# A hybrid decoder layer on one core: one residual add moved ahead of a normalisation on VectorE, and two blocks of router products reordered on TensorE

## The chip, the cores and the metric

The kernel runs on one core of one Trainium2 chip. The metric is the device time of one execution in microseconds; three runs of the kernel before are given. Everything is float32. A float32 product of TensorE appears in the profile as two matmul records (an output of 128x512 as "128x512 f32 x2").

## The reference

One step of one decoder layer, for 256 prompt tokens and 8 sample tokens (264 rows, D = 1024): RMSNorm, one input projection, dilated attention and RWKV-7 mixing side by side, a gated merge, an output projection with residual add; then RMSNorm, and a mixture of 32 experts of which each token takes four. What follows the merge is what matters here:

```
x = x + mixed @ w_out
h = rmsnorm(x, ln2)
logits = h @ w_router + b_router              # (264, 32)
top_v, top_i = top_k(logits, 4);  gate = softmax(top_v)
# per expert e, for the tokens that chose it:
gu  = h @ w_gate_up[e] + b_gate_up[e]         # 1024 -> 2048
act = (min(max(up, -7), 7) + 1) * (gt * sigmoid(1.702 * gt)),  gt = min(gt, 7)
x  += gate[e] * (act @ w_down[e] + b_down[e]) # 1024 -> 1024
y = rmsnorm(x, ln_f)
```

## The kernel before

The program of each engine is written out by hand, in its own block: TensorE (`pe`), VectorE (`dve`), ScalarE (`act`), GpSimd (`pool`), and SyncE (`sp`), which issues nearly all loads. No scheduler changes the order; an engine runs its instructions as they are written, and `wait_ge` on a semaphore holds back everything behind it on that engine.

The 264 rows form three tiles: m = 0 and 1 with 128 prompt rows each, m = 2 with the 8 sample rows. They are treated in the order `MORDER` = (2, 0, 1), so norm2(0) is the second RMSNorm of tile 2, norm2(1) that of tile 0, norm2(2) that of tile 1; residual(m) and logits(m) take the tile itself.

PSUM has eight banks. The list `psum_jobs` gives each product a bank in turn; `give(job)` waits until the job before in this bank is read out, `done` tells that the bank is full, `take` waits for that, and `free` tells that it is read out.

Around the change the work is as follows.
- Output projection: `out_projection(m, g)` makes 128 rows by 512 columns of `mixed @ w_out` (8 products, line 1550). VectorE adds it to the residual stream `acc` in `residual(m)` (a 128x512 add for each g, line 811). The sample tile has its own packed product (line 1578), and four adds of 8x512.
- Norm: ScalarE squares `acc` and takes the root (`rms2`, lines 659 and 660), VectorE takes the reciprocal (line 1105) and scales into `h2` (line 1106). Before rms2 of tile 0, ScalarE waits for the h2 of the sample rows and copies these rows of `acc` (line 671).
- Router: TensorE transposes h2 in blocks of 128 columns (`h2_T`, line 1246), ScalarE copies the result out (line 515), TensorE multiplies with w_router (`logits`, line 1569), VectorE takes the four largest (`route`, lines 1115 to 1118, semaphore `sel_r`), ScalarE the exponentials, VectorE the gates (`gates`, lines 1133 to 1135, semaphore `gate`).
- Ranks: products of the selection with constant matrices count the tokens ahead of each one for its expert (job `rk`, lines 1611 to 1622). From them VectorE builds `sel` (line 1153), which says which token sits in which of 64 slots of an expert.
- Sample gates: they are transposed and placed (lines 1616 and 1618) in bank BX, and read from there by ScalarE and VectorE.
- `open_sum(m, g)` (line 1601) copies a 128x512 piece of `acc` by a product with the identity into a PSUM bank, in which the experts' results are summed later.
- `gather` (line 1637) brings the tokens of an expert pair into the slots, `bias` (line 1646) opens the sums of the expert product.
- Expert loop: 32 turns (line 1686 gate and up, line 1697 transposes, line 1714 down, line 1669 the combination of the expert before).

The weights of an expert come in six units of 2 MB, four of w_gate_up and two of w_down, into a ring of eight buffers. The issue of unit n waits for the semaphore `unit_used` to reach n + 1 (line 489); the loop raises it by one for each unit that TensorE has consumed, and ahead of the loop it is raised by 3, 3 and 2 as buffers that held other weights come free, the last two behind wo10 and wo11.

Of the kernel before, what the change touches and what calls it, by code (L numbers as in the profile page):

```python
# [19 lines left out]
NB = 8  # L20
# [12 lines left out]
NE = 32  # L33
# [92 lines left out]
def build(nc, A, O):  # L126
# [5 lines left out]
    BG, BU, BY, BX = [bank[j] for j in ("rk", "ro1", "ht11", "ht10")]  # L132
    BA = ((bank["ro2"], bank["ro0"]), (bank["ht01"], bank["wo11"]))

    with ExitStack() as ctx:
# [3 lines left out]
        def sem(name):  # L139
            return ctx.enter_context(nc.semaphore(name))  # L140
# [3 lines left out]
        PS = [ctx.enter_context(nc.psum_tensor(f"ps{b}", [128, 512], F32)) for b in range(8)]  # L144
# [19 lines left out]
        C = {n: mats[:, i, :] for i, n in enumerate(CONST_NAMES)}  # L164
# [142 lines left out]
        gate = place(NM, NE)  # L307
# [18 lines left out]
        def S_(name):  # L326
            if name not in SEM:
                SEM[name] = sem(name)
            return SEM[name]

        def take(eng, job):
            eng.wait_ge(full[bank[job]], turn[job])

        def after(eng, *names):
            for job in names:
                eng.wait_ge(evac[bank[job]], turn[job])

        def psum(job, *dims, parts=128):
            return view(PS[bank[job]], 0, *dims)[:parts]
# [466 lines left out]
        def _(dve):  # L806
# [3 lines left out]
            def tt(out, a, b, op):  # L810
                return v.tensor_tensor(out, a, b, op)  # L811
# [276 lines left out]
            def residual(m):  # L1088
                n = ROWS[m]
                a = lambda g: acc[:n, m, g * 512:(g + 1) * 512]  # L1090
                if m == 2:
                    take(dve, "wo2")
                    for j in range(4):
                        ins = tt(a(j % 2), PS[bank["wo2"]][32 * j:32 * j + n, :], a(j % 2), ALU.add)
                        V.free(ins, "wo2") if j == 3 else V(ins)
                else:
                    for g in range(2):
                        take(dve, f"wo{m}{g}")
                        V.free(tt(a(g), psum(f"wo{m}{g}", 512, parts=n), a(g), ALU.add), f"wo{m}{g}")

            def norm2(i):
                m = MORDER[i]
                n = ROWS[m]
                dve.wait_ge(S_("rms2"), i + 1)
                V(v.reciprocal(rs1[:n, m:m + 1], rs1[:n, m:m + 1]))
                V.ready(v.scalar_tensor_tensor(h2[:n, m, :], acc[:n, m, :], rs1[:n, m:m + 1], ln2b[:n], ALU.mult, ALU.mult),
                        "h2", i + 1)
# [11 lines left out]

            dve.wait_ge(S_("ld_acc"), 48)  # L1120
            residual(2)
            dve.wait_ge(S_("ld_ln2"), 16)
            norm2(0)
            residual(0)
            norm2(1)
            residual(1)
            def gates(i):
# [72 lines left out]
            last = dve.snap(passes * NE)  # L1200
# [29 lines left out]
        def _(pe):  # L1230
            mm = nc.tensor.matmul

            def give(job):

                if turn[job] > 1:
                    pe.wait_ge(evac[bank[job]], turn[job] - 1)

            def done(ins, job):
                ins.then_inc(full[bank[job]], 1)

            def transposes(job, pieces, width, parts=128):

                give(job)
                for n, src in enumerate(pieces):
                    rows = src.shape[0]
                    last = nc.tensor.transpose(PS[bank[job]][:parts, n * width:n * width + rows], src, C["ident"][:rows, :rows])  # L1246
                done(last, job)
# [80 lines left out]
            for h in range(H):  # L1328
# [4 lines left out]
                if h % 2:  # L1333
                    job = f"ov{h // 2}"
                    give(job)
                    for hh in (h - 1, h):
# [3 lines left out]
                        last = mm(psum(job, S)[q, 128:256], vn[:, 1, hh * 64:hh * 64 + 64], ptb[:, hh % 2, 256:384], start=False, stop=True)  # L1340
# [9 lines left out]
                if h == 3:  # L1350
# [3 lines left out]
                    for t in range(3):  # L1354
                        last = nc.tensor.transpose(PS[bank["sst"]][:64, KO[t]:KO[t] + KT[t]], scs[:KT[t], t, :], C["ident"][:KT[t], :KT[t]])
                    done(last, "sst")
                if h == 6:
# [3 lines left out]
                    for t in range(3):  # L1361
                        last = nc.tensor.transpose(PS[bank["spt"]][:KT[t], t * 64:t * 64 + 64], s64[:64, KO[t]:KO[t] + KT[t]], C["ident"][:64, :64])
# [7 lines left out]
            for c in range(4):  # L1370
                for g in range(2):
                    last = mm(psum("sv", 4, 2, 4)[:, c, g, :], pvm[:, g, c * 128:(c + 1) * 128], C["quad"][:, 0:4], start=True, stop=True)
# [35 lines left out]
            def prod(lhs, rhs):  # L1408
# [20 lines left out]
                                                     start=True, stop=True), "Auk")  # L1429
            heads("MT", prod(aA2, aI), "LX2", "X2T")  # L1430
            for pr in range(2):
                after(pe, f"MT{pr}", f"AV{pr}")
                for m in range(2):
                    job = f"HG{pr}{m}"
                    give(job)
                    for hh in range(4):
                        for r in range(2):
                            a, b = AV[half(r), pr, m, hh, :], natK[half(r), m, head(pr, hh)]
                            both = bass.AP(a.tensor, a.offset, [list(a.ap[0]), [b.offset - a.offset, 2], [1, 64]])
                            last = mm(psum(job, 4, 128)[half(r), hh, :], aA2T[half(r), pr, m, hh, :], both, start=True, stop=True)  # L1440
# [3 lines left out]
            for r in range(2):  # L1444
                job = f"Y0{r}"
                give(job)
                for m in range(2):
                    for hh in range(4):
                        for pr in range(2):
# [4 lines left out]
                            last = mm(out, HG[half(r), pr, m, hh, 0:64], aBrb[half(r), pr, m, hh, :], start=False, stop=True)  # L1454
                done(last, job)
            for r in range(2):
                job = f"Rp{r}"
                give(job)
                for m in range(2):
                    for hh in range(4):  # L1460
                        for pr in range(2):
                            last = mm(psum(job, 2, 4, 64)[half(pr), m, hh, :], HG[half(r), pr, m, hh, 64:128],
                                      aBrb[half(r), pr, m, hh, :], start=True, stop=True)
# [49 lines left out]
            for c in range(1, NCH):  # L1513
                job = f"yt{c}"
                give(job)
                for hh in range(4):
                    for pr in range(2):
                        last = mm(psum(job, 4, CH)[half(pr), hh, :], stc[c - 1][half(pr), hh, :], Rp[half(pr), hh, c * CH:(c + 1) * CH],
                                  start=True, stop=True)
# [16 lines left out]
            for c in range(4):  # L1536
                pe.wait_ge(S_("obT"), c + 1)
                for d in range(KD):
                    if c == 0:
                        give(f"mb{d}")  # L1540
                    last = mm(psum(f"mb{d}", T), wb[:, c, d * 128:(d + 1) * 128], YT[:, c, :], start=c == 0, stop=c == 3)  # L1541
# [12 lines left out]
            def half(rows, u, j):  # L1554

                return rows[:, u * 256 + j:u * 256 + 256:2]

            def h2_T(i):
                m = MORDER[i]
                pe.wait_ge(S_("h2"), i + 1)  # L1560
                for g in range(2):
                    transposes(f"ht{m}{g}", [half(h2[:ROWS[m], m, :], 2 * g + c // 2, c % 2) for c in range(4)], ROWS[m])

            def logits(m):
                n = ROWS[m]
                after(pe, f"ht{m}0", f"ht{m}1")
                give(f"ro{m}")
                for k in range(KD):
                    last = mm(psum(f"ro{m}", NE, parts=n), h2T[:, k, m * 128:m * 128 + n], wr[:, k, :], start=k == 0, stop=k == KD - 1)
                done(last, f"ro{m}")  # L1570
# [3 lines left out]
            for k in range(4):  # L1574
                pe.wait_ge(S_("mix"), 2 * k + 2)
                for j in range(4):
                    kk, g = 2 * k + j // 2, j % 2
                    last = mm(PS[bank["wo2"]][32 * j:32 * j + NB, :], mixT[:, kk, S:T], wo[:, kk, g * 512:(g + 1) * 512],
                              start=k == 0, stop=k == 3)
# [15 lines left out]
            def bank_free(b):  # L1595
                pe.wait_ge(evac[b], max(turn[j] for j in jobs if bank[j] == b))

            def open_sum(m, g):

                bank_free(BA[m][g])  # L1600
                mm(PS[BA[m][g]][:, :], C["ident"], acc[:, m, g * 512:(g + 1) * 512], start=True, stop=False)

            open_sum(1, 0)
            open_sum(1, 1)
            h2_T(2)
            open_sum(0, 0)
            logits(1)
            give("rk")
            rk = psum("rk", 3, NE)
            pe.wait_ge(S_("sel_r"), 2)  # L1610
            mm(rk[:, 0, :], C["before"], selr[:, 0, :], start=True, stop=False)
            mm(rk[:, 1, :], C["ones"], selr[:, 0, :], start=False, stop=False)
            mm(rk[:, 2, :], C["ones"], selr[:, 0, :], start=False, stop=False)
            pe.wait_ge(S_("gate"), 1)
            bank_free(BX)
            nc.tensor.transpose(PS[BX][0:NE, 0:NB], gate[:NB, 2, :], C["ident"][:NB, :NB])
            for g in range(2):
                last = mm(PS[BX][g * 64:g * 64 + 64, 64:64 + NE], C["idstack"][0:NB, 0:64], gate[:NB, 2, :], start=True, stop=True)
            last.then_inc(S_("gate_s_full"), 1)
            pe.wait_ge(S_("sel_r"), 3)  # L1620
            mm(rk[:, 1, :], C["before"], selr[:, 1, :], start=False, stop=False)
            done(mm(rk[:, 2, :], C["ones"], selr[:, 1, :], start=False, stop=True), "rk")
# [5 lines left out]
            for g in range(2):  # L1628
                q = slice(g * 64, g * 64 + NE)
                last = mm(PS[BY][g * 64:g * 64 + NB, :], gsT[q], yS[q, :], start=True, stop=True)  # L1630
# [27 lines left out]
            for m in range(2):  # L1658
                last = nc.tensor.transpose(PS[BY][0:NE, m * 128:(m + 1) * 128], gate[:, m, :], C["ident"])
# [67 lines left out]
            for m in range(2):  # L1727
                for g in range(2):
                    q = slice(g * 64, g * 64 + 64)
                    last = mm(PS[BA[m][g]][:, :], selgT[q, m * 128:(m + 1) * 128], yS[q, :], start=False, stop=True)  # L1730
                last.then_inc(S_("cmb_full"), 1)
            pe.wait_ge(S_("samp_sq"), 1)
            for g in range(2):
                last = mm(PS[BX][g * 64:g * 64 + 64, 0:1], C["idstack"][:, 0:64], sqs, start=True, stop=True)
# [23 lines left out]
```

## Time and profile before

| | us |
|---|---|
| median of three runs | 1331.39 |
| lowest, highest | 1330.75, 1335.32 |
| the profiled execution, its own time | 1331.39 |
| its span in the trace | 1329.5 |
| TensorE busy | 1222.0 (92%) |
| VectorE busy | 337.6 (25%) |
| ScalarE busy | 200.7 (15%) |
| mean granted TensorE clock, share of full | 0.981 |

The span is cut into three parts: the mixers and the projection up to about 380 us, the router up to about 400 us, and the 32 experts from there to the end. The page's view of 40 equal slices shows it for DMA:

```profile
DMA  8357565414498999999999999999999999999994
GB/s 276 122 176 170 195 212 143 146 35 166 164 390 333 427 429 427 429 429 427 429 429 427 429 429 427 429 429 427 429 429 427 429 430 427 429 430 427 429 429 173
```

Each column is 33.2 us. TensorE's busy share is an average over records that overlap, so it doesn't tell by itself that TensorE sets the end.

### The profile page before, as it was taken

The page shows a single profiled execution, that of the slowest core. Times are in us where ns is not written, and L with a number is a line of the kernel's source. Part 1 is how long each engine was busy: PE and PEld are TensorE (multiplying, and loading weights), DVE is VectorE, ACT ScalarE, POOL GpSimd, SP SyncE. Part 2 cuts the span into 40 slices and gives each one's busy share as a digit, 9 for nine tenths or more (in the row PEclk, how much of TensorE's full clock was granted, in tenths as well). Part 3 has the DMA queues.
Part 4 walks back from the last instruction along what each step waited for, and adds up shares of the span by engine and source line. Part 5 has one row for each costly group of instructions (what it writes and reads, how often), then busy time and mean ns, then how long its engine had stood idle before and what let it go on. Part 6 is the DMA issues. An engine that isn't in the chain of part 4 may idle for free.

```text
span 1329.5 us, 18567 instructions
## 1 busy us (share of the span) xinstructions
PE 1222.0 (92%) x7636; PEld 605.2 (46%) x7636; DVE 337.6 (25%) x649; ACT 200.7 (15%) x401; POOL 79.2 (6%) x48
## 2 busy tenths in 40 slices
PE   5999968898999999999999998999999989999996
PEld 5888854886553334333333333333333333333332
DVE  3042756735541112111211111121111112111112
ACT  2113423222121001001011000110010010101002
POOL 0000070550000000000000000000000000000001
PEclk9999987899989999999999999999999999999998
DMA  8357565414498999999999999999999999999994
GB/s 276 122 176 170 195 212 143 146 35 166 164 390 333 427 429 427 429 429 427 429 429 427 429 429 427 429 429 427 429 429 427 429 430 427 429 430 427 429 429 173
DMA packets 52510, 460.03 MB, mean 346 GB/s; under 512 B 7922, under 2 KB 10300, under 8 KB 27884
## 3 DMA queue, kind: packets, MB, share of 16 engines
q1 hardware_dynamic: 49252, 451.45, 82.1%
q0 software_dynamic: 1888, 5.34, 2.1%
q10 hardware_dynamic: 1328, 2.64, 0.6%
q8 instruction: 31, 0.51, 0.2%
q14 instruction: 11, 0.09, 0.0%
HBM read 454.27 MB, written 5.11 MB: 346 GB/s over the span
## 4 chain that ended last, share of the span: by engine, by line
PE 60%; DMA 27%; DVE 4%; issue 3%; ACT 3%; POOL 1%; SPq 1%; DVEq 0%; ACTq 0%; POOLq 0%
PE ps L1686 21%; DMA work<-in_w_gate_up 13%; DMA ring<-in_w_gate_up 13%; PE ps L1714 12%; PE ps L1271 8%; PE ps L1637 4%; PE ps L1669 2%; PE ps L1550 2%; PE ps L1246 2%; PE ps L1646 2%; PE ps L1490 1%; PE ps L1409 1%; POOL ring L761 1%; PE ps L1541 1%; DVE ring L811 1%
## 5 line engine op out<-in xcount | busy, mean ns | idle before, releaser
L1686 PE MATMUL ps<-ring,work 128*64 128x512 f32 x1536 | 341.8, 595 | 20.6 <-DMA ring<-in_w_gate_up 20.2
L1686 PEld LDWEIGHTS ps<-ring,work 128*64 128x64 f32 x1536 | 107.4, 137 | 252.2 <-issue 217.2
L1714 PE MATMUL ps<-ring,work 128*64 128x512 f32 x768 | 170.1, 595 | 18.4 <-ACT work L717 18.4
L1271 PE MATMUL ps<-work,ring 128*128 128x264 f32 x672 | 150.3, 386 | 0.7 <-DVE work L811 0.7
L1180 DVE TENSOR_SCALAR work<-ps 128x512 f32<-128x512 f32 x32 | 22.1, 692 | 466.9 <-PE ps L1686 466.9
L1271 PEld LDWEIGHTS ps<-work,ring 128*128 128x128 f32 x672 | 127.4, 190 | 22.5 <-DVE work L811 0.8
L1686 PE MATMUL ps<-work 128*64 128x512 f32 x512 | 114.3, 596 | 6.2 <-DMA work<-in_w_gate_up 6.2
L1714 PEld LDWEIGHTS ps<-ring,work 128*64 128x64 f32 x768 | 53.4, 137 | 119.7 <-issue 104.0
L1199 DVE SCALAR_TENSOR_TENSOR work<-work 128x512 f32<-128x512 f32 x32 | 24.1, 752 | 309.8 <-ACT work L720 309.8
L712 ACT ACTIVATE work<-work 128x512 f32<-128x512 f32 x32 | 20.1, 629 | 503.1 <-DVE work L1180 503.1
L1637 PEld LDWEIGHTS ps<-work 128*128 128x128 f32 x544 | 68.2, 200 | 29.9 <-DVE work L1184 15.2
L1637 PE MATMUL ps<-work 128*128 128x128 f32 x544 | 74.7, 292 | 2.0
L811 DVE TENSOR_TENSOR work<-work 128x512 f32<-128x512 f32 (+7 forms) x73 | 61.5, 843 | 50.8 <-ACT work L515 45.0
L1686 PEld LDWEIGHTS ps<-work 128*64 128x64 f32 x512 | 35.2, 137 | 84.3 <-issue 69.3
L1669 PE MATMUL ps<-work 64*128 64x512 f32 x256 | 63.6, 615 | 0.0
L802 POOL TENSOR_SCALAR work<-work 8x512 f32<-8x512 f32 x2 | 3.1, 1561 | 1011.4 <-DVE work L1221 1011.3
L1714 PE MATMUL ps<-work 128*64 128x512 f32 x256 | 56.7, 595 | 5.9 <-ACT work L717 5.9
L720 ACT ACTIVATE work<-ps 128x512 f32<-128x512 f32 x32 | 19.1, 597 | 230.6 <-PE ps L1714 230.6
L515 ACT ACTIVATE work<-ps 128x264 f32<-128x264 f32 (+6 forms) x63 | 26.5, 421 | 159.6 <-PE ps L1271 123.4
L1669 PEld LDWEIGHTS ps<-work 64*128 64x128 f32 x256 | 22.0, 186 | 41.1 <-issue 41.1
L1646 PE MATMUL ps<-work 32*64 32x512 f32 x264 | 35.9, 613 | 0.0
L1714 PEld LDWEIGHTS ps<-work 128*64 128x64 f32 x256 | 17.6, 137 | 39.9 <-issue 32.1
(250 smaller groups left out, 913.8 us busy)
## 6 DMA issues: line engine op xcount, KB each, us to landing
ring<-in_w_gate_up SPq DMA_DIRECT2D x96, 2048.0 KB, 31.1
ring<-in_w_down SPq DMA_DIRECT2D x48, 2048.0 KB, 35.2
work<-in_w_gate_up SPq DMA_DIRECT2D x32, 2048.0 KB, 30.9
work<-in_w_down SPq DMA_DIRECT2D x16, 2048.0 KB, 34.7
ring<-in_w_in SPq DMA_DIRECT2D x6, 3072.0 KB, 16.0
ring<-in_w_out SPq DMA_DIRECT2D x1, 4096.0 KB, 14.0
ring<-in_w_in SPq DMA_DIRECT2D x2, 1536.0 KB, 9.1
ring<-in_cache_k SPq DMA_DIRECT2D x16, 192.0 KB, 3.3
```

The costliest lines, as they stand in the source:

```text
L515: A_.free(nc.scalar.activation(dst, src, func, **kw), job)
L811: return v.tensor_tensor(out, a, b, op)
L1180: v.tensor_scalar(gt, PS[BG][:, :], LIMIT, None, ALU.min).then_inc(S_("gt"), 1)
L1199: v.scalar_tensor_tensor(accs, yS, gsamp[:, bass.ds(it, 1)], accs, ALU.mult, ALU.add).then_inc(S_("samp_out"), 1)
L1246: last = nc.tensor.transpose(PS[bank[job]][:parts, n * width:n * width + rows], src, C["ident"][:rows, :rows])
L1271: last = mm(psum(job, T), WIN[gi % 2][:, k, j * 128:(j + 1) * 128], hT[:, k, :], start=k == 0, stop=k == KD - 1)
L1550: last = mm(psum(job, 512), mixT[:, k, m * 128:m * 128 + 128], wo[:, k, g * 512:(g + 1) * 512], start=k == 0, stop=k == KD - 1)
L1637: last = mm(PS[BX][:, c * 128:(c + 1) * 128], h2[:, m, half * 512 + (c // 2) * 256 + c % 2:half * 512 + (c // 2 + 1) * 256:2], sel[:, m].r ...
L1646: mm(PS[(BG, BU)[i]][g * 64:g * 64 + 64, :], pick[q, :], ebias[q, g * 512:(g + 1) * 512], start=True, stop=False)
L1669: mm(PS[BA[m][g]][:, :], selgT[q, m * 128:(m + 1) * 128], yS[q, :], start=False, stop=False)
L1686: last = mm(PS[bnk][g * 64:g * 64 + 64, :], lhs, UNIT[n % 8][:, w0 + base + g * 512:w0 + base + (g + 1) * 512], start=False, stop=k == KD - 1)
L1714: last = mm(PS[BY][g * 64:g * 64 + 64, :], lhs, UNIT[n % 8][:, w0:w0 + 512], start=k == 0, stop=k == KD - 1)
```

## The change

On VectorE, residual(0) moves from behind norm2(0) to directly behind residual(2). On TensorE, logits(1) moves ahead of open_sum(0, 0), and the transpose and placement of the sample gates move ahead of `give("rk")` and the first three rank products. The list of PSUM jobs, ScalarE, GpSimd and SyncE are the same.

```
             residual(2)
+            residual(0)
             dve.wait_ge(S_("ld_ln2"), 16)
             norm2(0)
-            residual(0)
             norm2(1)
             residual(1)
...
             open_sum(1, 1)
             h2_T(2)
+            logits(1)
             open_sum(0, 0)
-            logits(1)
+            pe.wait_ge(S_("gate"), 1)
+            bank_free(BX)
+            nc.tensor.transpose(PS[BX][0:NE, 0:NB], gate[:NB, 2, :], C["ident"][:NB, :NB])
+            for g in range(2):
+                last = mm(PS[BX][g * 64:g * 64 + 64, 64:64 + NE], C["idstack"][0:NB, 0:64], gate[:NB, 2, :], start=True, stop=True)
+            last.then_inc(S_("gate_s_full"), 1)
+
             give("rk")
             rk = psum("rk", 3, NE)
             pe.wait_ge(S_("sel_r"), 2)
             mm(rk[:, 0, :], C["before"], selr[:, 0, :], start=True, stop=False)
             mm(rk[:, 1, :], C["ones"], selr[:, 0, :], start=False, stop=False)
             mm(rk[:, 2, :], C["ones"], selr[:, 0, :], start=False, stop=False)
-            pe.wait_ge(S_("gate"), 1)
-            bank_free(BX)
-            nc.tensor.transpose(PS[BX][0:NE, 0:NB], gate[:NB, 2, :], C["ident"][:NB, :NB])
-            for g in range(2):
-                last = mm(PS[BX][g * 64:g * 64 + 64, 64:64 + NE], C["idstack"][0:NB, 0:64], gate[:NB, 2, :], start=True, stop=True)
-            last.then_inc(S_("gate_s_full"), 1)
             pe.wait_ge(S_("sel_r"), 3)
```

VectorE's instructions between the end of the sample residual and the scaling of tile 0, as a difference (ps5 and ps6 hold the two halves of out_projection(0); the four adds ahead of them are residual(2)):

```order
 L811 TENSOR_TENSOR work<-ps4,work 8x512 x4
+L811 TENSOR_TENSOR work<-ps5,work 128x512
+L811 TENSOR_TENSOR work<-ps6,work 128x512
 L1105 RECIPROCAL work<-work 8x1
 L1106 SCALAR_TENSOR_TENSOR work<-work 8x1024
-L811 TENSOR_TENSOR work<-ps5,work 128x512
-L811 TENSOR_TENSOR work<-ps6,work 128x512
 L1105 RECIPROCAL work<-work 128x1
 L1106 SCALAR_TENSOR_TENSOR work<-work 128x1024
```

The two adds that read the first tile's projection stand ahead of the reciprocal and scaling of the eight sample rows now.

TensorE's instructions from the second half of the transposes of tile 1 to the last rank product, before (ps5 is the bank of open_sum(0, 0), ps1 that of logits(1), ps2 that of the ranks, ps7 that of the sample gates):

```order
 L1246 MATMUL ps0<-work 128x128 x4
 L1601 MATMUL ps5<-work 128x512
 L1569 MATMUL ps1<-work 128x32 x8
 L1611 MATMUL ps2<-work 128x32
 L1612 MATMUL ps2<-work 128x32
 L1613 MATMUL ps2<-work 128x32
 L1616 MATMUL ps7<-work 32x8
 L1618 MATMUL ps7<-work 64x32 x2
 L1621 MATMUL ps2<-work 128x32
 L1622 MATMUL ps2<-work 128x32
```

and in the changed kernel, where the lines behind 1601 have moved by up to 6 with the code:

```order
 L1246 MATMUL ps0<-work 128x128 x4
 L1569 MATMUL ps1<-work 128x32 x8
 L1601 MATMUL ps5<-work 128x512
 L1610 MATMUL ps7<-work 32x8
 L1612 MATMUL ps7<-work 64x32 x2
 L1618 MATMUL ps2<-work 128x32
 L1619 MATMUL ps2<-work 128x32
 L1620 MATMUL ps2<-work 128x32
 L1622 MATMUL ps2<-work 128x32
 L1623 MATMUL ps2<-work 128x32
```

The product of 512 columns stands behind the logits instead of ahead of them, and the gate pieces stand between it and the ranks.

## Rows read from the trace of the kernel before

**Rows 1.** Chain that ended last: start us, us, what.

```profile
738.23 33.07 DMA ring<-in_w_gate_up
1299.91 3.65 PE ps L1686 x16
```

**Rows 2.** Windows: from:to, length, busy (x instructions) by engine, clock, DMA share, GB/s.

```profile
390.00:392.00 2.00, 2.00 (x6) 0.36 (x7) 1.40 (x7) 1.15 (x6) 0.00 (x0) 0.56 0.96 397
396.00:398.00 2.00, 2.00 (x15) 1.20 (x13) 1.73 (x9) 0.54 (x1) 0.00 (x0) 0.73 0.14 57
402.00:404.00 2.00, 2.00 (x14) 0.58 (x10) 0.00 (x0) 1.41 (x3) 0.00 (x0) 1.00 0.00 0
440.00:480.00 40.00, 38.31 (x198) 15.65 (x196) 8.00 (x19) 4.54 (x9) 0.00 (x0) 1.00 1.01 428
```

**Rows 3.** Timeline of SyncE's queue at 380 and 404: start us, us, what.

```profile
380.68 0.91 SPq L489 DMA_DIRECT2D ring<-in_w_gate_up  x2
...
404.33 3.77 SPq L489 DMA_DIRECT2D ring<-in_w_gate_up  x2
```

**Rows 4.** Timeline of TensorE, output projection: start us, us, what.

```profile
349.73 14.00 PE L1550 MATMUL ps<-ring,work 128*128 128x512 f32 x32
363.66 1.12 PE L1246 MATMUL ps<-work 8*128 8x8 f32 x8
364.71 7.13 PE L1550 MATMUL ps<-ring,work 128*128 128x512 f32 x16
```

**Rows 5.** Timeline of VectorE, same stretch.

```profile
356.31 1.27 DVE L1106 SCALAR_TENSOR_TENSOR work<-work 8x1024 f32<-8x1024 f32 x1
...
363.84 0.69 DVE L811 TENSOR_TENSOR work<-ps,work 128x512 f32<-128x512 f32 x1 [5.53 <-PE ps L1550]
366.20 0.16 DVE L1105 RECIPROCAL work<-work 128x1 f32<-128x1 f32 x1 [1.67 <-ACT work L660]
366.40 1.28 DVE L1106 SCALAR_TENSOR_TENSOR work<-work 128x1024 f32<-128x1024 f32 x1
```

**Rows 6.** Timeline of ScalarE, the copies of the sample rows.

```profile
357.70 1.29 ACT L671 ACTIVATE work<-work 8x512 f32<-8x512 f32 x2 [1.71 <-DVE work L1106]
```

**Rows 7.** Timeline of TensorE, from the router to the first expert.

```profile
384.73 1.02 PE L1601 MATMUL ps<-work 128*128 128x512 f32 x2
385.83 1.94 PE L1569 MATMUL ps<-work 128*128 128x32 f32 x16
...
389.51 0.41 PE L1621 MATMUL ps<-work 128*128 128x32 f32 x2 [0.73 <-DVE work L1118]
...
389.98 1.79 PE L1601 MATMUL ps<-work 128*128 128x512 f32 x2
391.70 1.88 PE L1630 MATMUL ps<-work 32*8 32x512 f32 x4
393.51 3.75 PE L1637 MATMUL ps<-work 128*128 128x128 f32 x16
...
398.20 2.15 PE L1637 MATMUL ps<-work 128*128 128x128 f32 x16
...
400.50 1.08 PE L1686 MATMUL ps<-ring,work 128*64 128x512 f32 x4
```

**Rows 8.** Timeline of TensorE, the longest wait shortly before the change.

```profile
328.10 2.29 PE L1541 MATMUL ps<-work,ring 128*128 128x264 f32 x6 [4.49 <-issue]
```

**Rows 9.** Windows of two earlier stretches.

```profile
190.00:212.00 22.00, 15.09 (x52) 8.93 (x52) 18.38 (x32) 9.66 (x28) 6.85 (x2) 0.50 0.95 270
328.00:334.00 6.00, 5.90 (x19) 4.83 (x20) 5.76 (x8) 0.00 (x0) 0.00 (x0) 0.72 0.45 175
```

**Rows 10.** Timeline of VectorE, sel and the last gates.

```profile
391.27 1.12 DVE L1153 TENSOR_SCALAR work<-work 128x64 f32<-128x64 f32 x4
...
397.08 0.24 DVE L1135 TENSOR_SCALAR work<-work 128x32 f32<-128x32 f32 x1
```

## The prediction

> **What bounds the kernel now.** I read the chain of waits first, because the change sits in front of a long loop and only the chain says what that loop is worth. From 400 us on the kernel runs 32 experts, each with 12 MB of weights. Up to 738 us the chain runs on TensorE; from there it is made mostly of weight transfers, the first of 33.07 us, and the last of them releases TensorE at 1299.9 us, some 30 us before the end [rows 1]. So the end is set by the weight stream: a fixed number of bytes at a fixed rate, counted from the moment at which the stream last stood still.
>
> The windows show where that is. The DMA share falls to 0.14 in 396 to 398 us and is 0.00 in 402 to 404 us; in 440 to 480 us it is 1.01 at 428 GB/s, and the transfers in the chain say that it stays so [rows 1, 2]. The reason is the ring of eight weight buffers. Eight units were queued before the loop, the last two at 380.68 us; the ninth is issued at 404.33 us, when TensorE has consumed the first unit of the first expert [rows 3]. TensorE reaches this expert at 400.50 us [rows 7]. Therefore each microsecond by which TensorE enters the expert loop later or earlier moves the end by a microsecond, until the hole in the stream (396 to 404 us, some 8 us) is closed. The question is only what the change does to 400.50 us.
>
> **The change part by part.** There are two independent edits.
>
> First edit, VectorE: residual(0) now stands ahead of norm2(0). norm2(0) makes the eight sample rows of h2, which TensorE transposes (the eight L1246 at 363.66 us) between the two halves of the output projection. Before, its scaling (1.27 us) was over at 357.58 us, 6 us ahead of its reader, under out_projection(0, 0) and (0, 1), which run from 349.73 for 14.00 us [rows 4, 5]. residual(0) needs both of these products; its second half cannot start before TensorE has finished the second, and starts at 363.84 us [rows 5]. What was hidden now stands bare behind it: 363.84 + 0.69 (second half of the residual) + 0.16 (reciprocal, priced by the next one) + 1.27 (scaling) + 0.04 twice between them (366.20 + 0.16 to 366.40) = 366.04. With 0.1 us for the signal and the weight load in front of the first transpose, an estimate, that is 366.1 to 366.2. TensorE is in order and waits there from 363.66: **+2.5 us**. Queued behind the waiting transposes is out_projection(1, 0), 7.13 us [rows 4], and behind it everything up to the loop.
>
> The other engines follow, and I looked for a second delay. ScalarE waits for the same h2, copies the sample rows (1.29 us [rows 6]) and only then squares tile 0: it starts that at about 367.4 us instead of 364.6. From the square to VectorE's reciprocal it took 1.6 us before (366.20 [rows 5]), so norm2(1) ends near 370.5 us. Its reader, the transposes of tile 0, comes after out_projection(1, 0), at 366.18 + 1.1 + 7.1 = 374.3 us. That leaves 3.8 us: no second stall. The last two weight units are issued 2.5 to 4 us later than 380.68, while the first six (12.6 MB, 29 us at 428 GB/s from 357 us) are still under way until 386: nothing. The gain that one might look for in the first edit, banks of PSUM freed earlier, is nothing either: TensorE shows no wait for such a bank in this stretch.
>
> TensorE's clock adds a term. The nearest rows of a stall are those before 328.10 us, 4.49 us of idleness [rows 8]; the granted clock behind it is 0.72 over 328 to 334 us [rows 9], and as the clock has only the levels 2.4 and 1.2 GHz, (1 - 0.72) x 2 x 6 = 3.4 us of these are at 1.2. On the other side, short waits in the loop (1.7 us of 40 not busy) leave the clock at 1.00 [rows 2]. The new stall of 2.5 us has 1.05 us of transposes of eight columns directly behind it, so it is nearer to the former. A spell of 3.4 us at half clock over dense work loses 1.7 us. The bounds are 0 (none) and 3.4 us (6.8 us at half clock, the length of the spell near 391 us, below). I take **+1.7**, with a little over even odds.
>
> The Trainium skill says in "TensorE: Matmul & The Clock Gate", part 1, "the default state is throttled, and activity releases the throttle". By that rule the stall can cost more than its own length, and the sum is the +1.6 below; with no loss of clock it would be -0.1. The trace of before agrees with the direction: half clock follows its pauses.
>
> Second edit, TensorE: logits(1) moves ahead of open_sum(0, 0), and the transpose and the two placements of the sample gates move ahead of the first three rank products. open_sum used to fill the 0.9 us in which ScalarE evacuates the transposed rows (L1601 at 384.73, logits at 385.83 us [rows 7]). Now TensorE is idle there, logits(1) starts at the same time, and open_sum(0, 0) takes its 0.9 us after it. Before, TensorE had done three rank products and the gate pieces and waited 0.73 us until 389.51 for the third selection from VectorE [rows 7]. The moved open_sum fills this wait: the last rank product comes at most 0.2 us later. VectorE's route and gates don't wait for any of it and keep their pace, and sel, which the gather needs, is ready at 392.39 us (391.27 + 1.12) as before [rows 10]: **0** in the first place.
>
> But again the clock. In before, the stretch 385.8 to 390.0 us holds only products of 32 columns or fewer and the wait, and at 390 to 392 us the granted clock is 0.56, at 396 to 398 us 0.73, so at 1.2 GHz from 390.2 to 397.1, 6.8 us [rows 2]. In it the open_sum took 1.79 us (1.02 at 384.73), the sample bias 1.88 and the gather 3.75 (2.15 for the next one at full clock) [rows 7]. After the change the thin stretch is cut by a dense product in its middle. If that keeps the clock at 2.4 GHz, open_sum and bias end at about 392.1; the gather waits for sel and starts at 392.5 instead of 393.51 (-1.0) and takes 1.6 us less: **-2.6 us**. More isn't to be had: the gates of tile 1 are ready at 397.32 us, just under the new entry at 397.9 [rows 10]. If the spell comes all the same the term is 0 to +0.2. I take -2.6 at about two to one; the change leaves less thin work together than before, but adds 0.9 us of idleness next to it.
>
> Sum: 2.5 + 1.7 - 2.6 = **+1.6 us** on the end. The profiled execution took 1331.39 us (span 1329.5 and 1.9 around it), and that is also the median of the three runs. Forecast: **1333.0 us**.
>
> **The rivals.** What a measurement of this kernel can tell from no change is about 0.5%, or 6.7 us; nearly all cases below lie within it.
> - A, the forecast: stall, one short spell at half clock behind it, the later spell gone. 1333.0 us, chance 0.36.
> - B, no spell behind the stall, the later one gone: 2.5 - 2.6 = -0.1, 1331.3 us. For it: the stall is little more than half as long as the one before 328.10 us. Chance 0.28.
> - C, a spell in both places: 2.5 + 1.7 + 0.2 = +4.4, 1335.8 us. For it: clock changes follow pauses with some scatter, and the second edit opens a new pause of 0.9 us. Chance 0.18.
> - D, a spell only in the later place: +2.7, 1334.1 us. Chance 0.13.
> - E, slower than can be overlooked: the clock doesn't come back within 3.4 us but stays at half over the whole of out_projection(1, 0), as it stayed for 22 us at 190 to 212 us [rows 9]. Price: 2.5 + 7.1 (that projection doubled) + 0.2 = +9.8, 1341.2 us. It decides the verdict once more than some 8 us of dense work run at half clock. Against it: in that stretch TensorE was busy for 15.1 of 22 us in small pieces, whereas here 7 us of dense products follow at once. Chance 0.04.
> - F, faster by over 0.5%: the hole in the weight stream is 8 us, so it isn't excluded by the bandwidth, but no term gives more than -2.6 us. Even without the stall (VectorE's order forbids that) the time would be 1328.8 us, 0.2% less; only a long spell at half clock that the profile of before doesn't show could bring more. Chance 0.01.
> - That the shift doesn't reach the end at all (the stream has slack somewhere else) gives 1331.4 us as B does. Against it is the DMA share of 1.01 right behind the hole.
>
> **How the numbers follow.** The likeliest is A, so 1333.0. A to D lie from 1331.3 to 1335.8; with 1.3 us below for a spell in the profile of before that other runs may not have, and 1 us above for two spells longer than taken, the range is 1330.0 to 1336.8. Faster 0.01 (F), slower 0.04 (E), the same 0.95.
>
> **What would show it.** In the profile after: the eight transposes of the sample rows start 2.4 to 2.6 us after the second product of out_projection(0), with VectorE named as releaser; VectorE's scaling of eight rows comes after the two residual halves. No wait of TensorE before the transposes of tile 0. A clock under 1.00 somewhere in 366 to 371 us in case A or C, and none between the logits of tile 1 and the expert loop in A or B. The entry into the expert loop at 402.1 (A), 400.4 (B), 404.9 (C) or 403.2 us (D), the ninth weight unit issued 3.8 us later, and the last transfer's end moved by the same amount. The prediction is wrong in its core if the entry moves and the end doesn't, or if the entry moves by more than 6 us.

## The result and the profile after

| | before | after |
|---|---|---|
| median, us | 1332.08 (16 runs) | 1339.05 (16 runs) |
| lowest to highest | 1328.23 to 1336.39 | 1337.70 to 1341.85 |
| mean granted TensorE clock, profiled execution | 0.981 | 0.977 |
| ratio after / before | | 1.0051, 95% interval 1.0041 to 1.0060 |

The change costs 7 us, 0.51%. I had forecast +1.6 us and a range up to 1336.8, so the time lies outside. Of the 6.05 us between the forecast of 1333.0 and the median of 1339.05, 0.7 us is the base: I had counted from 1331.39, three runs, and the median of 16 is 1332.08. The other 5.4 us is the change itself, +7.0 instead of +1.6.

The profiled execution of the changed kernel took 1340.89 us, 9.5 us more than that of before. 2.5 us of these lie ahead of everything that the change touches: out_projection(0, 0) starts at 352.24 us instead of 349.73. This start varies from execution to execution: over the eleven profiles of this case it lies between 343.94 and 352.69 us, and at both ends of this for one and the same kernel (e4 and e7 below). All positions are therefore counted from the start of out_projection(0, 0) from here on, called P. The expert loop is entered at P + 50.77 before and P + 57.78 after: +7.01 us, which is the whole of the loss. The names in the rows: ps is a bank of PSUM, work and ring are buffers in SBUF, and L1550 is a line of kernel.py; behind line 1601 the numbers differ by up to 6 from those of before, as the code has moved. TensorE's timeline of the changed kernel, answering to [rows 4, 7] (start us, us, what, and in brackets the idle time before and who ended it):

```profile
352.24 14.00 PE L1550 MATMUL ps<-ring,work 128*128 128x512 f32 x32
368.59 1.12 PE L1246 MATMUL ps<-work 8*128 8x8 f32 x8 [2.35 <-DVE work L1106]
369.64 10.05 PE L1550 MATMUL ps<-ring,work 128*128 128x512 f32 x16
...
393.68 1.94 PE L1569 MATMUL ps<-work 128*128 128x32 f32 x16 [0.95 <-ACT work L515]
395.46 1.52 PE L1601 MATMUL ps<-work 128*128 128x512 f32 x2
...
397.39 0.64 PE L1618 MATMUL ps<-work 128*128 128x32 f32 x2
...
399.11 0.61 PE L1623 MATMUL ps<-work 128*128 128x32 f32 x2
399.54 2.05 PE L1601 MATMUL ps<-work 128*128 128x512 f32 x2
401.52 1.88 PE L1631 MATMUL ps<-work 32*8 32x512 f32 x4
403.33 3.44 PE L1638 MATMUL ps<-work 128*128 128x128 f32 x16
```

The reader is to see three things. The transposes of the sample rows wait 2.35 us for VectorE's scaling; they stand at P + 16.35 instead of P + 13.93, 2.42 us later. out_projection(1, 0) behind them takes 10.05 us instead of 7.13: 2.92 us. And the stretch from logits(1) at 393.68 to open_sum(0, 1) at 399.54 takes 5.86 us, where it took 4.15 before (385.83 to 389.98 [rows 7]): another 1.7 us. The five rank products start 0.43 us apart (397.39 to 399.11) in it, where at full clock they stand 0.22 us apart (e6 below shows it). With the new order and full clock the stretch takes 4.30 us (e2 below), so 0.15 of the 1.7 us is the order and 1.56 the clock. 2.42 + 2.92 + 1.7 = 7.0.

VectorE in the same execution, answering to [rows 5, 10]:

```profile
366.35 0.69 DVE L811 TENSOR_TENSOR work<-ps,work 128x512 f32<-128x512 f32 x1 [6.17 <-PE ps L1550]
367.07 0.15 DVE L1105 RECIPROCAL work<-work 8x1 f32<-8x1 f32 x1
367.26 1.27 DVE L1106 SCALAR_TENSOR_TENSOR work<-work 8x1024 f32<-8x1024 f32 x1
371.55 0.16 DVE L1105 RECIPROCAL work<-work 128x1 f32<-128x1 f32 x1 [3.02 <-ACT work L660]
371.75 1.28 DVE L1106 SCALAR_TENSOR_TENSOR work<-work 128x1024 f32<-128x1024 f32 x1
...
399.84 0.42 DVE L1150 SCALAR_TENSOR_TENSOR work<-ps,work 128x32 f32<-128x32 f32 x2 [1.20 <-PE ps L1623]
400.29 1.12 DVE L1153 TENSOR_SCALAR work<-work 128x64 f32<-128x64 f32 x4
```

and the instruction of line 1150 in the kernel before:

```profile
390.82 0.42 DVE L1150 SCALAR_TENSOR_TENSOR work<-ps,work 128x32 f32<-128x32 f32 x2
```

The second half of the residual, reciprocal and scaling follow each other without a hole, as worked out. New is the wait of 1.20 us for the last rank product. It costs nothing, though: `sel` (line 1153) is ready at 401.41, and the gather that needs it starts at 403.33, directly behind the sample bias on TensorE. The 1.7 us are TensorE's own, spent in its queue at half clock.

The windows of the changed kernel, answering to [rows 2] (from:to, length, busy by engine, granted clock, DMA share, GB/s):

```profile
366.00:368.00 2.00, 0.24 (x1) 0.00 (x0) 1.58 (x3) 0.00 (x0) 0.00 (x0) 1.00 1.00 426
368.00:376.00 8.00, 7.41 (x16) 3.74 (x17) 1.98 (x3) 3.10 (x7) 0.00 (x0) 0.57 1.01 430
376.00:394.00 18.00, 17.05 (x80) 9.68 (x79) 4.74 (x16) 4.24 (x8) 0.00 (x0) 1.00 0.99 411
396.00:406.00 10.00, 10.00 (x35) 5.79 (x34) 6.55 (x30) 1.57 (x7) 0.00 (x0) 0.50 0.44 184
406.00:408.00 2.00, 2.00 (x16) 1.07 (x15) 1.44 (x8) 0.54 (x1) 0.00 (x0) 0.94 0.00 0
```

Behind the stall the clock is 0.57 over 8 us: (1 - 0.57) x 2 x 8 = 6.9 us at 1.2 GHz; in the profile of before the clock is 1.00 from P + 14 to P + 40.5. In the router it is 0.50 for all of 396 to 406 us and a little beyond, 10.2 us where [rows 2] gave 6.8. It begins 3.2 us later from P than before (P + 43.8 against P + 40.5), but earlier in the program: in open_sum(0, 0), ahead of the rank products, and not behind them. And the end follows the entry:

```profile
413.86 3.77 SPq L489 DMA_DIRECT2D ring<-in_w_gate_up  x2
```

```profile
1309.43 3.65 PE ps L1687 x16
```

The first is SyncE's issue of the ninth weight unit (404.33 before [rows 3]; +9.5 with the 2.5 of the late start), the second the piece of the chain released by the last weight transfer (1299.91 before [rows 1]). From the entry into the loop to this piece are 1309.43 - 410.02 = 899.41 us after, and 1299.91 - 400.50 = 899.41 us before.

### The profile page after: what moved, and what is told of

It reads as the page before. It is cut to its first block, busy times and chain, and to the rows that moved or that the text cites. A ratio compares the mean times of both kernels' runs of the same rounds, so it can differ in the third digit from the quotient of the medians.

```text
span 1339.0 us, 18567 instructions
## 1 busy us (share of the span) xinstructions
PE 1229.0 (92%) x7636; PEld 609.7 (46%) x7636; DVE 337.6 (25%) x649; ACT 200.9 (15%) x401; POOL 79.1 (6%) x48
## 4 chain that ended last, share of the span: by engine, by line
PE 61%; DMA 27%; DVE 4%; issue 3%; ACT 3%; POOL 1%; SPq 1%; DVEq 0%; ACTq 0%; POOLq 0%
PE ps L1687 20%; DMA work<-in_w_gate_up 13%; DMA ring<-in_w_gate_up 13%; PE ps L1715 12%; PE ps L1271 8%; PE ps L1638 4%; PE ps L1550 2%; PE ps L1670 2%; PE ps L1647 2%; PE ps L1246 2%; PE ps L1409 1%; PE ps L1490 1%; PE ps L1541 1%; DVE ring L811 1%; ACT work L689 1%
## 5 line engine op out<-in xcount | busy, mean ns | idle before, releaser
L811 DVE TENSOR_TENSOR work<-work 128x512 f32<-128x512 f32 (+7 forms) x73 | 61.5, 842 | 52.9 <-ACT work L515 47.1
L1687 PEld LDWEIGHTS ps<-work 128*64 128x64 f32 x512 | 35.2, 137 | 84.3 <-issue 69.3
L1246 PE MATMUL ps<-work 128*128 128x128 f32 (+4 forms) x141 | 22.3, 311 | 15.2 <-DMA work<-in_r_k 12.8
```

Source lines behind the costliest of these rows:

```text
L1687: last = mm(PS[bnk][g * 64:g * 64 + 64, :], lhs, UNIT[n % 8][:, w0 + base + g * 512:w0 + base + (g + 1) * 512], start=False, stop=k == KD - 1)
```

## The experiments

My theory after the result: the first edit costs the stall (2.4) and 2.9 for half clock behind it; the remaining 1.7 is the clock in the router. What it doesn't tell is to which edit the last term belongs. "Entry" is the first product of the expert loop from P in the one profiled execution; the timed ratio is against the kernel before, run beside it on the same chip; its median there was 1332.87 us (29 runs, for e1 to e4), 1331.83 (23, for e5 to e8) and 1332.78 (17, for e9), so the medians of the table can't be subtracted across these groups.

| kernel | entry | half clock behind P + 14 | median, us (runs) | ratio, 95% interval |
|---|---|---|---|---|
| before | 50.77 | 6.8 us from P + 40.5 | 1332.08 (16) | |
| after | 57.78 | 6.8 from 16.5, 10.2 from 43.8 | 1339.05 (16) | 1.0051, 1.0041 to 1.0060 |
| e1, VectorE's edit alone | 54.55 | 6.8 from 16.4, 3.4 from 47.1 | 1335.20 (12) | 1.0021, 1.0009 to 1.0034 |
| e2, TensorE's edit alone | 49.10 | none | 1330.95 (12) | 0.9981, 0.9969 to 0.9993 |
| e3, stall covered | 49.11 | none | 1329.72 (12) | 0.9980, 0.9971 to 0.9989 |
| e4, stall filled | 51.69 | none | 1337.53 (7) | 1.0042, 1.0027 to 1.0058 |
| e7, e4 once more | 58.13 | 17.1 from 40.5 | 1341.30 (1) | |
| e5, shift without stall | 57.58 | 10.2 from 43.9 | 1338.59 (6) | 1.0060, 1.0037 to 1.0082 |
| e6, router filled | 54.45 | 6.8 from 16.5 | 1334.64 (12) | 1.0027, 1.0014 to 1.0040 |
| e8, e2 with early load | 48.26 | none | 1329.74 (12) | 0.9981, 0.9971 to 0.9992 |
| e9, e8 with router filled | 48.24 | none | 1329.59 (12) | 0.9975, 0.9964 to 0.9986 |

The third column is worked out from the granted clock over windows of each trace.

**e1, VectorE's edit alone.** The kernel before with

```
             residual(2)
+            residual(0)
             dve.wait_ge(S_("ld_ln2"), 16)
             norm2(0)
-            residual(0)
```

> Only the first edit: residual(0) ahead of norm2(0), TensorE's order as before. My theory (the stall of 2.4 us and a spell at half clock behind it that costs 2.9 us belong to this edit; the other 1.7 us, in the router, to TensorE's order): the first product of the expert loop +5.3 us against before, measured from the start of out_projection(0, 0) (50.8 us before, so 56.1), and the end +5.3. Rival (everything follows from the stall, the router's 1.7 us too, because the stall shifts the router against the clock's falls): +7.0, 57.8 us. Rival from my forecast: +2.5 to +4.2.

TensorE's timeline in e1:

```profile
367.78 1.12 PE L1246 MATMUL ps<-work 8*128 8x8 f32 x8 [2.35 <-DVE work L1106]
368.83 10.02 PE L1550 MATMUL ps<-ring,work 128*128 128x512 f32 x16
...
397.00 1.10 PE L1601 MATMUL ps<-work 128*128 128x512 f32 x2
398.03 1.39 PE L1630 MATMUL ps<-work 32*8 32x512 f32 x4
399.48 3.26 PE L1637 MATMUL ps<-work 128*128 128x128 f32 x16
```

Stall and 10 us projection are here with the first edit alone, so 5.3 us belong to it. But entry is at 54.55, only +3.8 against before: open_sum(0, 1) takes 1.10 us instead of 1.79 and the sample bias 1.39 instead of 1.88; the fall comes 6.6 us later from P and lasts half as long. So my theory's 56.1 was 1.5 too high, and the rival's 57.8 further off; +3.8 does lie in the +2.5 to +4.2 of the rival from my forecast. The timed ratio gives +2.8 us (1.2 to 4.5 by its interval).

**e2, TensorE's edit alone.** The changed kernel with VectorE's order of before.

> Only the second edit: logits(1) ahead of open_sum(0, 0) and the gate pieces ahead of the rank products, VectorE's order as before. My theory now: the products of ranks fall into a spell at half clock that begins earlier, +1.7 us against before (52.5 us from the start of out_projection(0, 0) to the first product of the expert loop, 50.8 before). Rival from my forecast (the moved product of 512 columns keeps the clock up): -2.6 us, 48.2. Rival (the order is harmless by itself, only the stall does harm): 0 to +0.2, 50.8 to 51.0.

My new theory fell, and the forecast's view of this edit came back: alone it is a gain. Entry 49.10, -1.67 us, between the -2.6 of the forecast and no effect. The router of e2 at full clock:

```profile
376.00:400.00 24.00, 21.89 (x138) 14.04 (x138) 12.61 (x55) 7.99 (x20) 0.00 (x0) 1.00 0.94 398
```

and the two ends of the stretch from logits(1) to open_sum(0, 1), 4.30 us apart:

```profile
386.70 1.94 PE L1569 MATMUL ps<-work 128*128 128x32 f32 x16 [0.94 <-ACT work L515]
...
391.00 1.10 PE L1601 MATMUL ps<-work 128*128 128x512 f32 x2
```

The two edits are not additive: +3.8 and -1.7 in the profiles, +7.0 together; in the timed ratios 1.0021 x 0.9981 = 1.0002 against 1.0051. Something that neither has alone costs 5 to 6.5 us. That a single profile stands for its kernel here is borne out by the times: the twelve runs of e2 lie from 1326.67 to 1332.86, the sixteen of the changed kernel from 1337.70 up.

**e3, the stall covered.** The changed kernel with

```
+            out_projection(1, 0)
             h2_T(0)
-            out_projection(1, 0)
             h2_T(1)
```

> The changed kernel with out_projection(1, 0) issued ahead of the transposes of the sample rows, so that TensorE has 7 us of dense work while VectorE is late. Theory (stall and the spell behind it are the loss of the first edit): both are gone, -5.3 us against the changed kernel, 52.5 us from the start of out_projection(0, 0) to the expert loop, and against before 0 to +1.7. Rival (the late norm of the sample rows delays something else too, ScalarE's square of tile 0 above all): no more than -2.4 to -3 against the changed kernel.

Entry 49.11, 8.7 us less than the changed kernel; I had expected 5.3 less. VectorE's order is still the changed one; as soon as TensorE has 7 us of work while VectorE is late, all of the loss is gone, the router's part too. The rival about ScalarE is refuted. Whether the router is spared because the stall is gone or because it no longer runs 5.3 us later, e3 can't tell; e5 can.

**e4 and e7, the stall filled.** The changed kernel with, ahead of `h2_T(0)`,

```
+            give("wo10")
+            for _ in range(3):
+                mm(psum("wo10", 512), mixT[:, 0, 128:256], wo[:, 0, 0:512], start=True, stop=True)
```

> The changed kernel with three extra products of 512 columns (the first product of out_projection(1, 0), whose bank is written anew afterwards) in the place of the stall: TensorE is as late as before (2.6 us of extra work where it waited 2.4) but not idle. Theory (2.9 us of the loss are the clock's): TensorE's out_projection(1, 0) takes 7.1 instead of 10.05 us, and the kernel is 2.7 us faster than the changed one. Rival (the longer product time comes from something else that the late residual brings, a port or a transfer): it stays at 10 us and the kernel as slow as the changed one.

In the profile the projection is back at 7.1 us:

```profile
357.78 2.74 PE L1587 MATMUL ps<-ring,work 128*128 128x512 f32 x6
360.45 1.12 PE L1246 MATMUL ps<-work 8*128 8x8 f32 x8
361.50 7.13 PE L1550 MATMUL ps<-ring,work 128*128 128x512 f32 x16
```

So the 2.9 us are the clock's and nothing else's: same products, same late residual, but no idleness. The 2.7 us that I expected in the time did not come: the ratio is 1.0042 (1.0027 to 1.0058), which can't be told from the 1.0051 of the changed kernel. The six other runs took 1336.4 to 1340.4, 10 to 14 us more than this profiled execution (1326.4), which had reached P 6 us early. A second profile of the same kernel, e7, shows where they lose:

> The kernel of the dense filling in place of the stall once more, for one more profile: its first profile showed 1326.4 us and a mean clock of 0.990, its six timed runs 1336.4 to 1340.4 us and 0.974 to 0.980. Theory (the timed runs lose to the clock in the router, which the shift by the filling brings): out_projection(1, 0) at 7.1 us, a stretch at half clock between 40 and 52 us after the start of out_projection(0, 0), entry at 55 us. Rival (they lose before the projection): entry at 51.7 us and more half clock before it.

```profile
376.00:392.00 16.00, 15.06 (x78) 8.97 (x77) 4.74 (x16) 4.55 (x8) 0.00 (x0) 1.00 1.01 428
394.00:410.00 16.00, 16.00 (x60) 9.76 (x59) 7.71 (x36) 2.11 (x8) 0.00 (x0) 0.50 0.30 125
```

The projection was at full clock (7.13 us again) and the router at half for 17.1 us; entry 58.13. That is what seven of the eight executions of this kernel look like by their time. It lies 3 us later than the 55 that I expected. Against e2 (49.10) a delay of the router by 2.6 us of dense work, with no stall in it, thus cost 9 us in this execution and 2.6 us in the profile of e4. (VectorE's order differs from e2 as well, but e3 has the same order and enters at 49.11.)

**e5, a shift without a stall.** e2 (which had a full clock in the router) with six such products, 5.3 us, ahead of `h2_T(0)`.

> Only the second edit (TensorE's order of the changed kernel, VectorE's as before), and six extra products of 512 columns (5.25 us of dense work into a bank that is written anew afterwards) ahead of the transposes of the sample rows. So the router runs 5.3 us later, as it does in the changed kernel, but without a stall. The first product of the expert loop came 49.10 us after the start of out_projection(0, 0) with the second edit alone and 57.78 us in the changed kernel. Theory (the shift alone puts the router's thin products where the clock falls): 54.35 + 3.4 = 57.8, and a stretch at half clock from 44 us on. Rival (the stall itself, or the half clock before, makes the later fall likelier): 54.4, clock full in the router.

This experiment decides whether the stall is needed. TensorE in e5:

```profile
395.17 0.19 PE L1613 MATMUL ps<-work 8*32 8x8 f32 x1
395.29 0.42 PE L1615 MATMUL ps<-work 8*64 8x32 f32 x4
395.65 0.64 PE L1621 MATMUL ps<-work 128*128 128x32 f32 x2
396.09 0.62 PE L1622 MATMUL ps<-work 128*128 128x32 f32 x2
```

and its windows:

```profile
376.00:394.00 18.00, 17.06 (x90) 10.50 (x88) 4.85 (x17) 5.62 (x10) 0.00 (x0) 1.00 1.00 419
396.00:404.00 8.00, 8.00 (x27) 4.79 (x27) 5.20 (x22) 1.54 (x7) 0.00 (x0) 0.50 0.39 163
```

Entry 57.58 (57.8 expected, 54.4 by the rival), 10.2 us at half clock from P + 43.9: the router of the changed kernel to within 0.2 us, without a stall and without half clock before it. All six runs, 1337.38 us and up, lie above all twelve of e2. So neither the stall nor the half clock behind it is needed: that the router runs 5.3 us later is enough to bring the fall, and the first edit makes it run 5.3 us later.

**e6, the router filled.** The changed kernel with, between `h2_T(2)` and `logits(1)`,

```
+            bank_free(BA[0][0])
+            mm(PS[BA[0][0]][:, :], C["ident"], acc[:, 0, 0:512], start=True, stop=True)
```

> The changed kernel with one extra product of 512 columns (open_sum(0, 0) made twice, the first result is overwritten) in the 0.95 us in which TensorE waits for ScalarE ahead of logits(1). Theory (the wait and the thin products together make the clock fall in the router; 10.2 us at half clock in the changed kernel): the fall comes later or not at all, entry into the expert loop at 54.4 us after the start of out_projection(0, 0) instead of 57.78, 3.4 us faster than the changed kernel. Rival (one dense product of 0.9 us is too little, the rank products set it): no change, 57.8.

```profile
391.56 1.02 PE L1607 MATMUL ps<-work 128*128 128x512 f32 x2
392.66 1.94 PE L1569 MATMUL ps<-work 128*128 128x32 f32 x16
394.44 1.11 PE L1601 MATMUL ps<-work 128*128 128x512 f32 x2
...
396.51 0.39 PE L1624 MATMUL ps<-work 128*128 128x32 f32 x2
396.73 0.39 PE L1625 MATMUL ps<-work 128*128 128x32 f32 x2
396.95 1.11 PE L1601 MATMUL ps<-work 128*128 128x512 f32 x2
```

One dense product of 1.02 us in the 0.95 us hole that the second edit opens, which leaves logits(1) at P + 41.45 (41.44 in the changed kernel), and the rank products stand 0.22 us apart again: entry 54.45. In the timed runs the ratio goes from 1.0051 to 1.0027, which is 3.2 us. So the later place of the router doesn't bring the fall by itself in every case: with the hole filled the clock held in this execution. Four of the twelve runs were still at 1337.9 to 1339.0, so the filling doesn't prevent it each time.

**e8, the early load.** e2 with `wait_ge(npass)` and the register load moved ahead of `gather(1)`.

> Only the second edit, and TensorE loads the number of passes (a register load that waits for VectorE's npass) ahead of the second gather instead of behind the transposes of the gates. With the second edit alone TensorE stood idle 0.89 us before the first product of the expert loop, 1.5 us after the last gate was ready (398.19 to 399.70 us). Theory (the load and what follows it on TensorE's sequencer take this time, and the load is most of it): entry 0.5 to 0.9 us earlier, 48.2 to 48.6 us instead of 49.10, and the time 0.5 to 0.9 us lower. Rival (the branch into the loop takes it, or ScalarE's last copy, which ends at 399.16 us): 49.1 us.

In e2 TensorE had stood still ahead of the loop:

```profile
398.42 0.38 PE L1660 MATMUL ps<-work 128*32 128x128 f32 x2
399.70 2.79 PE L1687 MATMUL ps<-ring,work 128*64 128x512 f32 x12 [0.89 <-ACT work L689]
```

and in e8:

```profile
398.67 0.38 PE L1662 MATMUL ps<-work 128*32 128x128 f32 x2
399.11 3.23 PE L1687 MATMUL ps<-ring,work 128*64 128x512 f32 x14
```

Entry 48.26 instead of 49.10. The bracket in e2 names ScalarE's copy. But in e8 the same copy runs from 398.87 to 399.42 us, and the product starts at 399.11, before its end. The semaphore in front of the load wasn't it either: VectorE had written npass in e2 long before:

```profile
394.48 0.15 DVE L1160 CAST npass<-work 128x1 int32<-128x1 f32 x1
```

Of the two that were moved, the load is left, and moving it closed the hole. In the timed ratios the 0.8 us can't be told (0.9981 both).

**e9, all that helped.** e8 with the extra product of e6.

> The second edit without the first, with the early load of the number of passes and with the extra product ahead of logits(1). Theory: entry 48.3 us after the start of out_projection(0, 0), as with the early load alone, since the extra product lies in a wait; the router's stretch at half clock is gone in more runs, so that the median comes 0 to 1 us under that of the early load alone and 2.5 to 3.5 us under before. Rival (the extra product delays logits(1) or adds nothing): equal to or above the early load alone, 2.1 us under before or less.

Entry 48.24, ratio 0.9975 (0.9964 to 0.9986): 3.3 us faster than before, as expected, and about 10 faster than the changed kernel. Against e8 alone the intervals overlap, so whether the filling adds anything without the first edit stays open.

## Why the prediction was wrong

By its own steps:

- **The bound.** Right. From entry to the piece released by the last weight transfer it is 898.6 to 899.4 us in all eleven profiles, over entries that differ by 10 us from P. The end moves with the entry one to one.
- **The stall, +2.5.** Right: 2.42, on VectorE's steps as worked out. No second delay behind it: norm2(1) ended at P + 20.8, and its reader came at P + 27.3 without a wait.
- **The clock behind the stall, +1.7.** Mechanism right, size off: +2.9. I took the length of the nearest spell (3.4 us); it was 6.8 us, the other of my two ends, and e1, e6 and after all show 10.0 us for the projection. That end was priced at 3.4 us; 2.9 came of it, since 0.9 us of the spell lay over the transposes of the sample rows, which took 1.12 us at either clock. e4 shows that it is the clock alone.
- **The router, -2.6.** This is the step that failed. The prediction cut the problem at the entry to the router and priced the second edit there as if the router ran at its old time: the dense product in the middle of the thin stretch would keep the clock up. For this edit alone that is so (e2: no spell, though -1.67 and not -2.6). With the first edit ahead of it the router is 5.3 us later, and there the clock fell in the dense product itself, ahead of the rank products, and stayed down for 10.2 us: +1.7 where the sum has -2.6. The router thus costs 3.4 us more with the first edit than without it (+1.7 against -1.67). The 4.9 us by which the entries fail to add are these 3.4 and the 1.5 by which e1 came out under 5.3, its spell in the router being shorter. I had it as case C, "a spell in both places", but at +0.2 for the second spell: I let it be no worse than the old one, though nothing bounded its start. Here it reached back over the rank products, which TensorE works off at half the pace.
- **Second part of that step.** In e2 the -2.6 stopped at -1.67. The register load in front of the loop, which my sum leaves out, stood bare there: 1.5 us from the last gate to the first product. With the load moved (e8) the gain is 2.5.
- **The cases.** The outcome is C (18%) with both spells longer than priced: 2.42 + 2.92 + 1.7 = 7.0 instead of 2.5 + 1.7 + 0.2 = 4.4. The margin of 1 us above C "for two spells longer than taken" contradicts the bounds of the same text: with 3.4 for the first spell alone C would have been 1337.5. With the second at 10.2 us instead of 6.8 (another 1.7), the range would have had to reach 1339.

The rule of the Trainium skill, in "TensorE: Matmul & The Clock Gate", part 1, that activity releases the throttle, holds in e4 against after: idleness replaced by useless products gave 2.9 us back. For the router the runs don't bear it out as it stands: in e7 TensorE was busy for all of 394 to 410 us, and the granted clock was 0.50.

What stays open: what fixes the places at which the clock falls and comes back. In after and e5 it came back in the gather, in e7 only at the end of the second gather, with much the same products. One of eight executions of the e4 kernel, the one that reached P at 343.94 us, had no spell in the router at all. That the starts of the spells agree from P (16.5 in three profiles, 40.5 in two, 43.8 and 43.9) is seen, not explained. Nor is it shown how each kernel but e4's behaves in a second profile.

## What to carry to other kernels

Two reorderings that each look like a microsecond don't add where the clock of TensorE hangs on what stands around them: a stretch of small products that runs at full clock can fall to half when it merely starts 2.6 to 5.3 us later (e7, e5). Price such a stretch with the whole of its dependants, and try the edits one by one and together. Before an operation is moved ahead on one engine, look at what the moved one waits for: here a 128-row residual that waits for 14 us of products was put ahead of an 8-row scaling that TensorE needs first; giving TensorE a dense block to do meanwhile (e3) cost nothing and took the loss away.

## What the runs showed of the hardware that I had not expected

- 5.3 us of additional dense products made the kernel slower by more than 5.3 us: from e2 to e5, which differ in nothing else, the entry moves by 8.5 us (49.10 to 57.58) and the median, each against before beside it, by 8.7 us (-1.9 to +6.8). The ratios differ by 0.0079, which is 10.5 us, but one of the six runs of e5 took 1345.42 us at a mean clock of 0.939 and pulls its ratio up.
- A useless product in a wait can pay: one of 1.02 us took 3.3 us off the entry (57.78 to 54.45) and 3.2 us off the timed ratio.
- A wait that the profile puts down to one releaser (ScalarE's copy in e2) was in truth a register load on TensorE's own sequencer; only moving it told (49.10 to 48.26).
